# Up and convolution-in projections as seven quarter products each (Strassen's scheme), with the sums of weights made by GpSimd

## Chip, cores and metric

One NeuronCore of a Trainium2 chip runs one program. The metric is the time of the device in microseconds for the whole program, median over runs. Engine names are those of the profile: PE is TensorE's matmul side, PEld its weight loads, DVE is VectorE, ACT is ScalarE, POOL is GpSimd, SP is SyncE, which here only issues the loads of weights.

## What is computed

Two transformer-like layers and the start of a third on 512 tokens of width 1024, all in float32. The parts that the change touches:

```python
# end of layer 1: feed-forward
xn2 = rmsnorm(x, norm2_g[l])
x = x + jnp.square(jax.nn.relu(xn2 @ w_up[l])) @ w_down[l]      # w_up 1024 x 4096
# layer 2: gated short convolution, width 2048
h = rmsnorm_2(x, norm_g)
b, c, u, z = jnp.split(h @ w_in, 4, axis=-1)                    # w_in 1024 x 8192
vp = jnp.pad(c * u, ((0, 0), (CONV_WIDTH - 1, 0), (0, 0)))
conv = conv_w[0] * vp[:, 0:S] + conv_w[1] * vp[:, 1:1 + S] + conv_w[2] * vp[:, 2:2 + S]
x = x + (b * conv * jax.nn.silu(z)) @ w_out
```

Before them stand a dilated attention and a retention (with the input projection of 12,800 columns, two output projections and `w_out`), after them the key, value and query projections and a block-sparse attention of the third layer.

## The kernel before

Activations lie transposed in SBUF: feature on the partition, the 512 tokens along the free dimension (`xT`, eight slices k of 128 features). Every large matrix product is made of three fp32r matmuls: an operand is split into a high part (a rounded copy) and a low part (the value less its high part), and high x high, high x low and low x high are summed in one PSUM bank.

**Weights** come as chunks of 1 MB (128 x 2048 elements in SBUF) in a fixed list, `CHUNKS`. For each chunk SP loads it into one of three `raw` buffers, ACT writes the high part `wh` (`w_` of the scalar part, line 1167), DVE the low part `wl` (`w_` of the vector part, line 1618). `wh` and `wl` have two buffers each. `w_` of a chunk waits until PE has read the chunk that was two earlier (`chunk_read`).

**Products.** A chunk of `w_up` or of the convolution's `w_in` has 1024 rows and 256 columns. It gives two tiles ("col" form) of 128 output features x 512 tokens, each of 8 slices k x 3 matmuls, all of them with 128x128 stationary weights and 512 moving columns (`mm`, line 878). There are 8 chunks in each half of up (f = 0, 1) and 32 in the convolution, in the order c, u, b, z: 48 chunks of 48 matmuls.

**What follows a tile.** In up: DVE takes the relu and multiplies by the norm's factor `rs` out of PSUM (`up`), ACT squares it and writes its high part `hh` (line 1403), DVE writes the low part `hl` (line 1883). In the convolution, per tile: `c_` one DVE operation, `u` four (a product, one tap as a product with a scalar, two taps more), `b_` two, `z` three with a silu on ACT in between and a cast `cyh` on ACT (line 1416).

**Norms.** After each tile of `w_out`, down or the convolution's `w_out`, `add_x` adds it to `xT` and makes the next layer's input: `x * gain` on DVE, `xh` on ACT, `xl` on DVE. The squares' sums pass through a matmul (`sum_squares`) and give `rs`, which multiplies the results afterwards.

**Order.** All engines walk one list, `ORDER`, and each takes its own tokens from it in that order; semaphores (`tell`, `told`) do the rest. An engine that waits therefore holds all of its later tokens. `rooted` puts the norm's root some steps into the first two tiles (`ROOT`). POOL has one kind of token, `rate` (line 2183), in the last attention.

Of the kernel before, what the change touches and what calls it, by code (L numbers as in the profile page):

```python
# [14 lines left out]
S = 512  # L15
# [5 lines left out]
TURN = (1, 4, 4)  # L21
ATT_SCALE = 128 ** -0.5
NSA_SCALE = 64 ** -0.5

VECS = {}
# [6 lines left out]
NVEC = _at  # L32

# [81 lines left out]
def lay_out():  # L115
# [42 lines left out]
    for c in range(4):  # L158
        chunk(("wo", c), "w_out", 0, 8, c * 256, 256)
        for j in range(2):  # L160
            col(("wo", c, j), ("wo", c), j * 128, 8, ("y",), "out_d")
    for f in range(2):
        for c in range(8):
            chunk(("up", f, c), "w_up", 0, 8, f * 2048 + c * 256, 256)
            for j in range(2):
                col(("up", f, c, j), ("up", f, c), j * 128, 8, ("x", 1), "out_d")
        for c in range(8):
            chunk(("down", f, c), "w_down", f * 2048, 16, c * 128, 128)
            col(("down", f, c, 0), ("down", f, c), 0, 16, ("h", f), "out_d")
    for c in range(8):  # L170
        for n, part in ((1, "c"), (2, "u"), (0, "b"), (3, "z")):
            chunk((part, c), "a_w_in_2", 0, 8, n * 2048 + c * 256, 256)
            for j in range(2):
                col((part, c, j), (part, c), j * 128, 8, ("x", 2), "out_d")
# [28 lines left out]
SPLIT = [c[0] for c in CHUNKS if c[6] != "whole"]  # L203
# [14 lines left out]


# [5 lines left out]

def after_chunk(name):

    if name in LATE or name not in AFTER or AFTER[name] in PIECED:
        return []
# [41 lines left out]
def rooted(s, key, after):  # L271
# [5 lines left out]
    return o[:n] + flat(t[:at]) + [("sum_squares", s), ("root", s)] + o[n:] + flat(t[at:])  # L277

# [35 lines left out]
def make_order():  # L314
# [48 lines left out]
    for f in range(2):  # L363
        o += whole(("up", 1, 0, 0), ("up", 1, 0, 1)) if f else rooted(1, ("up", 0, 0, 0), ("up", 0, 0, 1))
        o += whole(*[("up", f, c, j) for c in range(8) for j in range(2)][2:])
        for k in range(8):
            o += whole(("down", f, k, 0)) + (squared(2, k) if f else [])
# [127 lines left out]
ROOT = {1: 5, 2: 4, 3: 0}  # L495
# [123 lines left out]
def program(nc, ctx, a, out):  # L619
# [10 lines left out]
    vec = sb("vec", [128, NVEC])  # L630
# [5 lines left out]
    wh = [sb(f"wh{i}", [128, 2048], F32R) for i in range(NSPLIT)]  # L636
    wl = [sb(f"wl{i}", [128, 2048], F32R) for i in range(NSPLIT)]
    tmp = [sb(f"tmp{i}", [128, S]) for i in range(4)]
    tmp45 = sb("tmp4", [128, 2, S])
    tmp += [tmp45[:, 0, :], tmp45[:, 1, :]]  # L640
# [3 lines left out]
    def v_(name, j=None):  # L644
        lo, hi = VECS[name]
        return vec[:, lo:hi] if j is None else vec[:, lo + j:lo + j + 1]
# [31 lines left out]
    with ExitStack() as ph:  # L678
        hh = sb("hh", [128, 16, S], F32R, ph)
        hl = sb("hl", [128, 16, S], F32R, ph)  # L680
    with ExitStack() as ph:
        cyh = sb("cyh", [128, 16, S], F32R, ph)
        cyl = sb("cyl", [128, 16, S], F32R, ph)
        vp = [sb(f"vp{i}", [128, S + 2], F32, ph) for i in range(2)]
        rs2 = sb("rs2", [128, S], F32, ph)
# [6 lines left out]
    with ExitStack() as ph:  # L692
# [7 lines left out]
        with ExitStack() as ph2:  # L700
            cn = sb("cn", [128, 1280], F32, ph2)
            w2 = sb("w2", [128, 2, 2, 64], F32, ph2)
# [8 lines left out]
    pair = [(sb(f"th{i}", [128, 2 * S], F32R), sb(f"tl{i}", [128, 2 * S], F32R)) for i in range(2)] + [(th2, tl2)]  # L711
    x_mid = nc.dram_tensor("x_mid", (4, 128, D), F32, kind="Internal").ap()
# [18 lines left out]

    XS = {"x": (xh, xl, "xl"), "or": (orh, orl, "orl"), "oa": (oah, oal, "oal"), "y": (yh, yl, "yl"),
# [5 lines left out]
    def new_rings():  # L738
# [5 lines left out]
                     main_n=Ring((7,), held), bo=Ring((0, 1, 2, 3), held))  # L744
# [49 lines left out]

    def x_event(s, k):
        return (("xT", 0, k), ("out_d", ("wo", k // 2, k % 2)), ("out_d", ("down", 1, k, 0)), ("out_d", ("ao", k, 0)))[s]
# [22 lines left out]
    def tensor(e):  # L819
# [27 lines left out]
        def mm(key, k):  # L847
# [33 lines left out]
            elif kk == kn - 1 and LAST[name] == key:  # L881
                m.then_inc(*tell("half", name))

# [255 lines left out]
        follow(x_in, x_raw, sum_squares, mm, turn_qk, scores, probs, values, mix_turn, mix_pick, mix, decay, ret, gated_ret,  # L1139
# [4 lines left out]
    def scalar(e):  # L1144
# [15 lines left out]
        def w_(j):  # L1160
# [3 lines left out]
            if name in BEFORE:  # L1164
                w.wait_ge(*told(*chunk_read(BEFORE[name])))
            for r, hi, _ in split_views(name, raw[SLOT[n]], wh[WSLOT[name]], wl[WSLOT[name]]):
                m = e.copy(hi, r)  # L1167
            m.then_inc(*tell("hi", name))

# [32 lines left out]
        def square(s, k):  # L1202
            w.wait_ge(*told(*x_event(s, k)))
            if k >= 3:
                w.wait_ge(*told("sum_square", s, k - 2))
# [8 lines left out]
            act(tmp[k % 2 if k else 5][:, :], xT[:, k, :], ACT.Square).then_inc(*tell("square", s, k))  # L1214

        def root(s):
# [3 lines left out]
            elif s == 3:  # L1220
                w.wait_ge(*told("out_d", ("z", 7, 1)))
# [163 lines left out]
        def gain(s, k, read):  # L1385
            w.wait_ge(*told("tile", read))
            w.wait_ge(*told("gain", s, k))
            e.copy(xh[:, k, :], tmp[2 + k % 3][:, :]).then_inc(*tell("xh", s, k))  # L1388

        def wo(c, j):  # L1390
            gain(1, c * 2 + j, ("gb", 3, 1))

        def up(f, c, j):
            key, n = ("up", f, c, j), c * 2 + j
            t = tmp[2 + n % 4]
            w.wait_ge(*told("out_d", key))
# [899 lines left out]
```

## Time and profile before

| | |
|---|---|
| median of 3 runs | 2085.94 us (2084.77 to 2087.73) |
| the profiled execution: time, span | 2087.92 us, 2086.1 us |
| mean granted TensorE clock | 0.991 |
| PE busy, matmuls | 2040.1 us (98%), 9591 |
| PEld busy | 1654.3 us (79%) |
| DVE busy | 1021.1 us (49%) |
| ACT busy | 769.2 us (37%) |
| POOL busy | 80.0 us (4%) |

Busy shares are over the whole span. A PE matmul's busy time in the rows overlaps the next one's, so the distance between two starts, not the mean duration, says what one costs. The engine that is busy 98% is waited for by the others in most of the span.

### The profile page before, as it was taken

The page shows a single profiled execution, that of the slowest core. Times are in us where ns is not written, and L with a number is a line of the kernel's source. Part 1 is how long each engine was busy: PE and PEld are TensorE (multiplying, and loading weights), DVE is VectorE, ACT ScalarE, POOL GpSimd, SP SyncE. Part 2 cuts the span into 40 slices and gives each one's busy share as a digit, 9 for nine tenths or more (in the row PEclk, how much of TensorE's full clock was granted, in tenths as well). Part 3 has the DMA queues.
Part 4 walks back from the last instruction along what each step waited for, and adds up shares of the span by engine and source line. Part 5 has one row for each costly group of instructions (what it writes and reads, how often), then busy time and mean ns, then how long its engine had stood idle before and what let it go on. Part 6 is the DMA issues. An engine that isn't in the chain of part 4 may idle for free. (4 is left out here: it accounts for less than half of the span.)

```text
span 2086.1 us, 22886 instructions
## 1 busy us (share of the span) xinstructions
PE 2040.1 (98%) x9591; PEld 1654.3 (79%) x9591; DVE 1021.1 (49%) x1353; ACT 769.2 (37%) x1217; POOL 80.0 (4%) x132
## 2 busy tenths in 40 slices
PE   8999999999999999999999999999999999999897
PEld 6899986778787888888888888888888777766566
DVE  4443444434343346643244455555554454856665
ACT  4564551332323323442143222222222214366763
POOL 0000000000000000000000000000000000033431
PEclk9999998999999999999999999999999999999999
DMA  5222122222222232333323333323333435210002
GB/s 201 73 69 81 61 81 71 81 86 81 86 81 81 81 101 89 93 101 101 101 89 94 101 101 91 103 89 101 101 89 94 124 96 160 65 41 21 31 21 61
DMA packets 186422, 181.32 MB, mean 87 GB/s; under 512 B 4816, under 2 KB 162896, under 8 KB 186320
## 3 DMA queue, kind: packets, MB, share of 16 engines
q1 hardware_dynamic: 182832, 172.41, 26.9%
q10 hardware_dynamic: 3488, 7.45, 1.3%
q8 instruction: 76, 1.25, 0.3%
q14 instruction: 26, 0.21, 0.0%
HBM read 173.56 MB, written 4.19 MB: 85 GB/s over the span
## 5 line engine op out<-in xcount | busy, mean ns | idle before, releaser
L878 PE MATMUL bank<-xh,wh 128*128 128x512 f32 x1352 | 549.4, 406 | 0.9 <-DVE wl L1618 0.8
L878 PE MATMUL bank<-xh,wl 128*128 128x512 f32 x1352 | 529.3, 391 | 0.0
L878 PE MATMUL bank<-xl,wh 128*128 128x512 f32 x1352 | 528.7, 391 | 0.0
L1618 DVE TENSOR_TENSOR wl<-raw,wh 128x2048 fp32r<-128x2048 f32 (+2 forms) x154 | 342.2, 2225 | 324.3 <-ACT wh L1167 324.3
L1167 ACT CAST wh<-raw 128x2048 fp32r<-128x2048 f32 (+2 forms) x154 | 285.1, 1854 | 383.6 <-PE bank L878 382.2
L878 PEld LDWEIGHTS bank<-xh,wh 128*128 128x128 f32 x1352 | 254.5, 188 | 61.6 <-issue 9.9
L878 PEld LDWEIGHTS bank<-xl,wh 128*128 128x128 f32 x1352 | 254.7, 188 | 57.5 <-issue 6.9
L878 PEld LDWEIGHTS bank<-xh,wl 128*128 128x128 f32 x1352 | 254.4, 188 | 54.9
L878 PE MATMUL bank<-wh,xh 128*128 128x512 f32 x512 | 214.4, 419 | 4.8 <-DVE xl L2140 4.6
L878 PE MATMUL bank<-wl,xh 128*128 128x512 f32 x512 | 202.0, 395 | 0.0
L878 PE MATMUL bank<-wh,xl 128*128 128x512 f32 x512 | 202.0, 395 | 0.0
L878 PEld LDWEIGHTS bank<-wh,xh 128*128 128x128 f32 x512 | 120.2, 235 | 18.2 <-issue 6.1
L878 PEld LDWEIGHTS bank<-wh,xl 128*128 128x128 f32 x512 | 120.1, 235 | 13.0
L878 PEld LDWEIGHTS bank<-wl,xh 128*128 128x128 f32 x512 | 121.1, 236 | 11.1 <-issue 0.2
L2183 POOL TENSOR_SCALAR tmp<-tmp,rs 128x128 f32<-128x128 f32 (+3 forms) x88 | 54.1, 627 | 1926.7 <-DVE rs L2104 1926.7
L1151 ACT ACTIVATE tmp<-tmp 128x512 f32<-128x512 f32 (+2 forms) x61 | 36.6, 603 | 194.8 <-DVE tmp L1580 100.6
L878 PE MATMUL bank<-hh,wh 128*128 128x512 f32 x256 | 99.6, 389 | 0.0
L878 PE MATMUL bank<-hl,wh 128*128 128x512 f32 x256 | 99.6, 389 | 0.0
L878 PE MATMUL bank<-hh,wl 128*128 128x512 f32 x256 | 99.6, 389 | 0.0
L1848 DVE TENSOR_TENSOR xT<-xT,bank 128x512 f32<-128x512 f32 x32 | 21.9, 686 | 122.4 <-PE bank L878 122.4
L2113 DVE TENSOR_TENSOR tl<-bank,th 128x512 fp32r<-128x512 f32 (+1 forms) x88 | 52.3, 636 | 42.7 <-ACT th L1524 42.5
L1388 ACT CAST xh<-tmp 128x512 fp32r<-128x512 f32 x24 | 14.9, 620 | 149.9 <-DVE tmp L1857 149.9
(256 smaller groups left out, 2578.8 us busy)
## 6 DMA issues: line engine op xcount, KB each, us to landing
raw<-in_w_in SPq DMA_DIRECT2D x50, 1024.0 KB, 5.1
raw<-in_a_w_in SPq DMA_DIRECT2D x32, 1024.0 KB, 5.7
raw<-in_w_up SPq DMA_DIRECT2D x16, 1024.0 KB, 5.4
raw<-in_w_down SPq DMA_DIRECT2D x16, 1024.0 KB, 6.0
raw<-in_w_proj_b SPq DMA_DIRECT2D x8, 1024.0 KB, 5.1
raw<-in_a_w_out SPq DMA_DIRECT2D x8, 1024.0 KB, 6.0
raw<-in_w_out SPq DMA_DIRECT2D x4, 1024.0 KB, 5.3
raw<-in_w_kv SPq DMA_DIRECT2D x4, 1024.0 KB, 5.1
```

Source lines behind the costliest of these rows:

```text
L878: m = e.matmul(o, p, q, start=k == 0 and n == 0, stop=k == K - 1 and n == 2)
L1151: return e.activation(o, i, f, scale=scale, **kw)
L1167: m = e.copy(hi, r)
L1388: e.copy(xh[:, k, :], tmp[2 + k % 3][:, :]).then_inc(*tell("xh", s, k))
L1618: m = e.tensor_tensor(lo, r, hi, ALU.subtract)
L1848: e.tensor_tensor(xT[:, k, :], xT[:, k, :], tile_bank(key)[:, :], ALU.add).then_inc(*tell("out_d", key))
L2113: e.tensor_tensor(lo[:, o:o + m], bank_of("turn_n", ("turn_n", u, f))[:, 0:m], hi[:, o:o + m], ALU.subtract).then_inc(*tell("lo_n", u, f))
L2183: m = e.tensor_scalar(x, x, wt[:, 32 + c + j:33 + c + j], gts[:, qb, (p * 2 + f) * 4 + i0 + j, 1 + n:2 + n], ALU.mult, ALU.mult)
```

## The change

Each of the 48 chunks is treated as a 2 x 2 block matrix: rows 0 to 511 and 512 to 1023, columns 0 to 127 and 128 to 255. The input is cut likewise: features k < 4 and k >= 4, tokens 0 to 255 and 256 to 511. The product is then made of seven quarter products in Winograd's form of Strassen's scheme with 15 sums. A quarter product has 4 slices k x 3 matmuls with 256 moving columns: 84 matmuls for a chunk.

- Sums of the input (`x_parts`, three of four sums for each k >= 4 and one for each k < 4) are made once per norm, by DVE, and split by ACT and DVE into `xwh`, `xwl`.
- Sums of the weights: four for each chunk, 128x512 elements, by POOL (`ws`) into a new buffer `wsum`. High and low parts are made per product: seven casts of 128x512 on ACT (`wq`) and seven subtractions on DVE (`wl_`). Products lie in a ring of eight places in `wh`, `wl`, `wsum`.
- Sums of the results, 128x256 each: ACT copies out of PSUM (`m1`, `m5`, `m4`), DVE sums (`u2`, `u3`, `c12`, `c11`), POOL sums in SBUF (`u4`, `c22`, `c21`). They build the two tiles in SBUF, and what follows (`up_rs`, `u`, `b_`, `z`) reads them there and not in PSUM.
- The tokens that follow a product come a fixed number of products later (`SEVEN_AT`); the weights are prepared 7, 6 and 5 products ahead.
- The middle tap's product with a scalar goes from DVE to ACT (`tap`). Chunks of `w_out` and the order of down are paired (0, 4, 1, 5, ...), so that slices k and k + 4 come together (`PAIRS`).
- To make room in SBUF six of the eight slices of `xT` are written to DRAM when the convolution begins and read back at its end (`x_keep`, `x_back`). The root of the norm comes after three products. PSUM banks 0 to 6 form the ring of the products.

```diff
-            chunk(("up", f, c), "w_up", 0, 8, f * 2048 + c * 256, 256)
-            for j in range(2):
-                col(("up", f, c, j), ("up", f, c), j * 128, 8, ("x", 1), "out_d")
+            chunk(("up", f, c), "w_up", 0, 8, f * 2048 + c * 256, 256, "seven")
...
+def sevens(r, s=None):
+    run, near = RUNS[r], NEXT_TO[r]
+    Q = 7 * len(run)
...
+    for q in range(7, Q):
+        name, n = product_at(r, q)
+        for what in ("ws", "wq", "wl"):
+            if q >= 8 or what == "wl":
+                due[max(0, q - SEVEN_AT[name[0], what])].append((what, name, n))
...
-    o += rooted(2, ("c", 0, 0), ("c", 0, 1))
-    o += whole(*[(part, c, j) for c in range(8) for part in "cubz" for j in range(2)][2:])
+    o += sevens(2, 2) + [("x_back", n) for n in range(3)]
...
+    for _w, _n in (("ws", 7), ("wq", 6), ("wl", 5), ("m1", 0), ("m5", 1), ("u2", 3), ("u4", 4), ("u3", 5), ("c22", 6), ("c12", 6),
+                   ("c11", 7), ("m4", 7), ("c21", 8), ("up_rs", 9), ("up", 11), ("up_lo", 13), ("u", 9), ("tap", 11),
+                   ("taps", 13), ("b", 9), ("z", 9), ("silu_z", 11), ("cy", 13), ("cyl", 15)):
...
+        def wm(name, n):                                        # PE
...
+            for k in range(4):
...
+                for x, (p, q) in enumerate(((hi, h), (hi, l), (lo, h))):
+                    m = e.matmul(product_bank(name, n), p[:, k, :], q, start=k == 0 and x == 0,
+                                 stop=k == 3 and x == 2)
...
+        def wq(name, n):                                        # ACT
...
+            e.copy(product_weights(name, n)[1], product_source(name, n)).then_inc(*tell("hi", name, n))
...
+        def wl_(name, n):                                       # DVE
+            _, hi, lo = product_weights(name, n)
+            w.wait_ge(*told("hi", name, n))
+            if n in (1, 2):
+                w.wait_ge(*told("rated", name, n + 1))
+            e.tensor_tensor(lo, product_source(name, n), hi, ALU.subtract).then_inc(*tell("lo", name, n))
...
+        def ws(name, n):                                        # POOL
+            if n in (0, 5, 6):
+                return
+            i, o = PLACE[name], product_weights(name, n)[0]
+            w.wait_ge(*told(f"raw{SLOT[i]}", i))
+            w.wait_ge(*told(*place_free(name, n)))
+            if n == 1:
+                m = e.tensor_tensor(o, raw_part(name, 1, 0), raw_part(name, 1, 1), ALU.add)
+            elif n == 2:
+                w.wait_ge(*told("rated", name, 1))
+                m = e.tensor_tensor(o, product_weights(name, 1)[0], raw_part(name, 0, 0), ALU.subtract)
...
+        def u4(name):                                           # POOL
...
+            e.tensor_tensor(t[:, 256:512], u2_sum, m5_copy, ALU.add).then_inc(*tell("rated", name, "u4"))
...
+        def up_rs(f, c, j):                                     # DVE
+            key, t = ("up", f, c, j), tmp[2 + (c * 2 + j) % 4]
+            tile_made(("up", f, c), j)
+            w.wait_ge(*told("rs", 1))
+            stt(t, t, 0.0, rs[:, :], ALU.max, ALU.mult).then_inc(*tell("out_d", key))
```

## Rows read from the trace of the kernel before

**Rows 1.** The page: busy time of each engine.

```profile
PE 2040.1 (98%) x9591; PEld 1654.3 (79%) x9591; DVE 1021.1 (49%) x1353; ACT 769.2 (37%) x1217; POOL 80.0 (4%) x132
```

**Rows 2.** PE's waits, longest in total first, with the longest single one.

```profile
PE bank L833 <- DVE xs L1598: 10.4, 4, 7.8
...
PE bank L878 <- DVE wl L1618: 1.5, 3, 0.7
```

**Rows 3.** Windows of up's first half and the convolution: engines' busy time, clock, DMA.

```profile
859.00:944.30 85.30, 85.01 (x374) 69.73 (x373) 42.22 (x40) 34.85 (x41) 0.00 (x0) 1.00 0.34 97
...
1206.30:1554.40 348.10, 348.10 (x1535) 287.91 (x1534) 184.84 (x197) 82.31 (x66) 0.00 (x0) 1.00 0.33 97
```

**Rows 4.** Timeline of PE, the convolution: start, duration, 512 moving columns.

```profile
1499.78 0.39 PE L878 MATMUL bank<-xl,wh 128*128 128x512 f32 x1
...
1502.96 0.39 PE L878 MATMUL bank<-xh,wh 128*128 128x512 f32 x1
```

**Rows 5.** Timeline of PE, last attention: fp32r matmuls of 256 moving columns.

```profile
2035.22 0.28 PE L1131 MATMUL bank<-th,v 128*128 128x256 f32 x1
...
2037.01 0.28 PE L1131 MATMUL bank<-tl,v 128*128 128x256 f32 x1
2037.13 0.39 PE L878 MATMUL bank<-wh,xh 128*128 128x512 f32 x1
```

**Rows 6.** Groups of DVE by shape: count, busy us, mean ns, idle before.

```profile
L1618 DVE TENSOR_TENSOR wl<-raw,wh 128x2048 fp32r<-128x2048 f32 x145 | 332.2, 2291 | 313.7 <-ACT wh L1167 313.7
...
L1883 DVE TENSOR_TENSOR hl<-tmp,hh 128x512 fp32r<-128x512 f32 x32 | 22.1, 692 | 43.3 <-ACT hh L1403 43.3
...
L2058 DVE TENSOR_TENSOR tmp<-tmp,rs 128x256 f32<-128x256 f32 x8 | 3.4, 425 | 0.3
```

**Rows 7.** Groups of ACT by shape.

```profile
L1167 ACT CAST wh<-raw 128x2048 fp32r<-128x2048 f32 x145 | 276.6, 1907 | 382.3 <-PE bank L878 382.2
...
L1403 ACT CAST hh<-tmp 128x512 fp32r<-128x512 f32 x32 | 19.9, 621 | 1.1
...
L1151 ACT ACTIVATE tmp<-tmp 128x256 f32<-128x256 f32 x8 | 3.3, 418 | 30.6 <-DVE tmp L2058 30.6
```

**Rows 8.** Timeline of POOL: its operation undisturbed, two of 128x512, eight of 128x128.

```profile
1910.09 1.53 POOL L2183 TENSOR_SCALAR tmp<-tmp,rs 128x512 f32<-128x512 f32 x2 [2.39 <-DVE rs L2104]
...
1843.53 3.44 POOL L2183 TENSOR_SCALAR tmp<-tmp,rs 128x128 f32<-128x128 f32 x8 [1843.09 <-DVE rs L2104]
```

**Rows 9.** Timeline of POOL and DVE where both work, four places.

```profile
1937.60 1.88 POOL L2183 TENSOR_SCALAR tmp<-tmp,rs 128x512 f32<-128x512 f32 x2 [4.13 <-DVE rs L2104]
...
1937.41 0.67 DVE L1624 TENSOR_TENSOR wl<-raw,wh 128x512 fp32r<-128x512 f32 x1
1938.00 1.28 DVE L2096 TENSOR_REDUCE rs<-bank 128x4 f32<-128x512 f32 x2
...
2045.37 2.40 POOL L2183 TENSOR_SCALAR tmp<-tmp,rs 128x512 f32<-128x512 f32 x2 [2.42 <-DVE rs L2104]
...
2045.19 1.27 DVE L1624 TENSOR_TENSOR wl<-raw,wh 128x512 fp32r<-128x512 f32 x2
...
1953.65 4.31 POOL L2183 TENSOR_SCALAR raw<-raw,rs 128x128 f32<-128x128 f32 x8 [1.95 <-DVE rs L2104]
...
1954.75 0.75 DVE L2134 TENSOR_TENSOR oT<-oT 128x512 f32<-128x512 f32 x1
1956.74 0.90 DVE L2140 TENSOR_TENSOR xl<-oT,xh 128x512 fp32r<-128x512 f32 x1 [1.24 <-ACT xh L1548]
...
1909.91 1.26 DVE L2096 TENSOR_REDUCE rs<-bank 128x1 f32<-128x512 f32 x2
```

**Rows 10.** Timeline of DVE where the convolution's input is made.

```profile
1205.80 0.69 DVE L1848 TENSOR_TENSOR xT<-xT,bank 128x512 f32<-128x512 f32 x1 [4.28 <-PE bank L878]
1206.52 0.49 DVE L1857 TENSOR_SCALAR tmp<-xT,vec 128x512 f32<-128x512 f32 x1
1207.69 0.69 DVE L1859 TENSOR_TENSOR xl<-tmp,xh 128x512 fp32r<-128x512 f32 x1 [0.69 <-ACT xh L1388]
```

More of the change, by code:

```diff
@@ L158, in lay_out @@
     for c in range(4):
[L159 removed]
+        chunk(("wo", c), "w_out", 0, 8, c * 128, 256, "far")
         for j in range(2):
@@ L171, in lay_out @@
         for n, part in ((1, "c"), (2, "u"), (0, "b"), (3, "z")):
-            chunk((part, c), "a_w_in_2", 0, 8, n * 2048 + c * 256, 256)
-            for j in range(2):
-                col((part, c, j), (part, c), j * 128, 8, ("x", 2), "out_d")
+            chunk((part, c), "a_w_in_2", 0, 8, n * 2048 + c * 256, 256, "seven")
     for c in range(8):
@@ L202 @@
 PLACE = {c[0]: n for n, c in enumerate(CHUNKS)}
-SPLIT = [c[0] for c in CHUNKS if c[6] != "whole"]
+SPLIT = [c[0] for c in CHUNKS if c[6] not in ("whole", "seven")]
 SLOT = []
@@ L277, in rooted @@
     return o[:n] + flat(t[:at]) + [("sum_squares", s), ("root", s)] + o[n:] + flat(t[at:])
+PIECES = ("m1", "m5", "u2", "u4", "u3", "c22", "c12", "c11", "m4", "c21")
+POST = {"up": ("up_rs", "up", "up_lo"), "c": (), "u": ("u", "tap", "taps"), "b": ("b",),
+        "z": ("z", "silu_z", "cy", "cyl")}
+def sevens(r, s=None):
+    run, near = RUNS[r], NEXT_TO[r]
+    Q = 7 * len(run)
+    due = [[] for _ in range(Q + 30)]
+    for i, name in enumerate(run):
+        for what in PIECES:
+            due[7 * i + SEVEN_AT[name[0], what]].append((what, name))
+    if s is not None:
+        due[ROOT[s]] += [("sum_squares", s), ("root", s)]
+    for q in range(7, Q):
[3 more added lines that the diff above has]
+                due[max(0, q - SEVEN_AT[name[0], what])].append((what, name, n))
+    due[Q - 4].append(("w", NTH[near[2]]))
+    due[Q].append(("w", NTH[near[3]]))
+    for i, name in enumerate(run):
+        for what in POST[name[0]]:
+            for j in range(2):
+                due[7 * i + SEVEN_AT[name[0], what] + j].append((what, *name[1:], j))
+    return flat([([("wm", *product_at(r, q))] if q < Q else []) + due[q] for q in range(Q + 30)])
 def placed(seq, extra):
@@ new lines, in tap, with silu_z @@
+        def tap(c, j):
+            f = c * 2 + j
+            w.wait_ge(*told("cu", c, j))
+            w.wait_ge(*told("rs", 2))
+            w.wait_ge(*(told("cyl", f - 4) if f >= 4 else told("xl", 2, 11)))
+            act(tmp[2 + f % 4], vp[j][:, 2:], ACT.Copy, scale=v_("a_conv_w_2", 32 + f)).then_inc(*tell("out_a", "tap", f))
+        def silu_z(c, j):
+            w.wait_ge(*told("out_d", ("z", c, j)))
+            act(two[:, j, :], two[:, j, :], ACT.Silu).then_inc(*tell("z_silu", c * 2 + j))
```

419 lines of the change are left out of this document (311 added, 108 removed).

## Prediction

> **What bounds the kernel now.** I read the page first: PE is busy 98% of the span, no other engine more than half [rows 1]. Because a busy PE says little by itself, I read its waits next. The longest is 10.4 us and lies at the start of the program; for the splits of weights PE waits 1.5 us in all [rows 2]. Then the windows of the two stretches that the change touches. In up's first half and in the convolution the busy time of PE equals the window (85.0 of 85.3 us, 348.1 of 348.1) at a granted clock of 1.00, DVE is busy for half of it (42.2 and 184.8 us), ACT for 41% and 24%, POOL not at all [rows 3]. So these stretches, 48 chunks of weights, last as long as PE needs for its matmuls, and about 5 us per chunk lie free on DVE and all of the time on POOL. DMA engines are busy a third [rows 3], and the change loads the same weights.
>
> The timeline gives what one matmul costs: from 1499.78 to 1502.96 us stand 15 starts, 14 distances, 0.227 us each [rows 4]. The whole convolution gives the same: 348.1 us for 1536 matmuls, 0.2266. A chunk is 48 of them, 10.88 us, and the 48 chunks are 522 us, a quarter of the time. Nothing else of the program is meant to change.
>
> **PE's side of the change.** A chunk becomes 84 matmuls with 256 moving columns, each with its own weight load. The last attention has such matmuls, fp32r too: from 2035.22 to the next matmul at 2037.13 us there are 16, 0.1194 us each [rows 5]. Half the columns cost 53% of the time, since each matmul has a fixed part. 84 x 0.1194 = 10.03 us, which is 0.85 us less than now for a chunk and 41 us less for 48. Bounds: with half of the 0.2267 (no more fixed part than now per column) a chunk is 9.52 us; the 0.1194 was seen in bursts of 16 alone, and the gain is gone at 10.88 / 84 = 0.1295. I take 0.1194.
>
> **ACT's side.** Per chunk seven casts of 128x512 at 0.62 us [rows 7] are 4.3 us in place of one of 1.91. Copies out of PSUM of 256 columns have no row; the 256-column activation takes 0.42 [rows 7], three are 1.3 (I would take 0.3 to 0.6 each). Up adds two squares and two casts as now, 2.5 us, the convolution per chunk a half tap, a half silu and a half cast, under 1 us. Sum 8.1 us in up and under 7 in the convolution: below PE's 10.0, so ACT costs nothing as long as nobody holds it up; it is the thinner cover in up.
>
> **DVE's side.** Per chunk seven subtractions of 128x512 in place of one of 2.29 us. One lasts 0.69 us by its row [rows 6], but the next begins earlier: from 1937.41 to 1938.00 it is 0.59 [rows 9]. Seven are 4.1 us. Four sums of 128x256, 0.43 each [rows 6], 0.34 where they follow at once: 1.4 us. In up two times `up_rs` and `up_lo`, 2.4 us at 0.59. Sum 7.9 us (9.3 with the rows' full durations). In the convolution nine operations of 128x512 follow each of the two tiles of four chunks, 4.5 per chunk, 2.7 us: sum 8.2. DVE alone would be under 10.03 as well.
>
> **POOL's side.** Per chunk four sums of 128x512 and three of 128x256, each with two inputs. The trace has only its one-input operation: 1.53 us for two of 512, 3.44 for eight of 128, so 0.76 and 0.43 each [rows 8], that is a fixed 0.32 us and 0.86 ns per element. Lower bound of a two-input sum: the same, 0.76 for 512 and 0.54 for 256, 4.7 us per chunk. Upper bound: the second input is read after the first at the same rate, 1.20 and 0.76, 7.1 us per chunk. I take the upper one, for the row's per-element time is one element per step and these sums need two. POOL too is under 10.03.
>
> **Where it collides.** Each engine fits, but two of them don't fit together. The timeline shows POOL's operations beside DVE's. Beside reductions out of PSUM two of them take 1.53 us. Where a DVE subtraction with both inputs in SBUF has begun just before (1937.41), they take 1.88; where two such stand in a row from 2045.19 to 2046.46, they take 2.40, 0.88 more, which is the rest of DVE's pair (1.09 us from POOL's start at 2045.37) less 0.2 that still overlaps. And eight small ones stretch from 3.44 to 4.31, while DVE's two two-input operations in the same stretch take 0.75 and 0.90 in place of 0.69 [rows 8, 9]: both sides lost, 1.1 us together, about the length of the two DVE operations. The two engines take turns when both read SBUF and DVE has two inputs there. The Trainium skill says this as a rule (SBUF — State Buffer, "Who interferes with whom": a DVE instruction with two SBUF inputs contends with a GpSimd instruction that reads SBUF, and the second to start blocks in full); by this rule, the trace agrees at all the places that I looked at.
>
> So the sum to make is of turns. DVE in up: seven `wl_`, two `up_rs`, two `up_lo`, all with both inputs in SBUF (`up_rs` read PSUM before), 11 x 0.59 = 6.5 us; in the convolution 11.5 x 0.59 = 6.8 us. `u2`, `u3`, `c12`, `c11` read PSUM and don't count. POOL's seven: 7.1 us, less 0.15 each that overlapped in rows 9, gives 6.0. Sum of turns: 12.5 us in up, 12.8 in the convolution, against 10.03 that PE would need and 10.88 that it needs now. Perfect turns are not likely: `c12` on DVE waits for `u4` on POOL with the later `wl_` queued behind it, `ws` on POOL waits for its predecessor, `u4` for `u2` on DVE. I add 0.5 us, about a third of the four PSUM sums: 13.0 and 13.3 us per chunk. Bounds: with the cheap POOL sums (4.7 less 1.0) the turns are 10.2 to 10.5 us, below the 10.88 of now, PE nearly the bound; with 7.1 whole and DVE's four PSUM sums never beside POOL, 6.8 + 7.1 + 1.4 = 15.3 us.
>
> The Trainium skill has a price for POOL's sum (GPSIMD Engine Reference, "Performance versus the Vector engine"): 4.50 us for 2048 elements of two inputs. An estimate from that page, in proportion to the elements, is 1.12 us for 512 and 6.2 for a chunk's seven; no row here shows it, and with it the turns would be 0.9 us shorter per chunk and the forecast 43 us lower, 2160.
>
> **Between the runs.** `x_parts` makes for the last pair a gain, three sums of 256, ACT's casts of 768 and 512 and DVE's two subtractions. Now the chain from the last tile to `xl` is 2.6 us (1205.80 to 1208.38) [rows 10]; the new one is about 0.7 + 0.5 + 3 x 0.4 + 0.85 + 0.9 = 4.2. Products 0 and 1 need only k < 4 and cover 2.9 us; the third waits some 1.5 us, twice in the program. At the start and end of each run the weights of four products wait for the last chunk of the old kind: 0 to 2 us, three times. I take 6 us for all of it, bounds 2 and 15. The 1.5 MB to DRAM and back cost nothing: the DMA engines are a third busy [rows 3], nobody reads `xT` meanwhile, and the reload has the first tile of `w_out`, 10.9 us, before its sum needs it; if late by 4 us, DVE's slack in that stretch (half) takes it.
>
> **Sum.** Up 16 x 13.0 = 208, convolution 32 x 13.3 = 426, together 634 us against 522: +112, and +6 makes +118. On the profiled execution of 2087.9 us (span 2086.1 and 1.8 around it) that is 2206, and since it was 2 us above the median of the runs, I predict 2203 us.
>
> **Rivals.**
> - *Faster: PE stays the bound.* The turns cost little, because DVE's and POOL's waits fall into the 2 us that each has free, or POOL's sums are cheap. For it: each engine alone is under 10.03 us, and the weights are prepared 5 to 7 products (7 to 10 us) ahead, so single delays are absorbed. Against it: a lead absorbs delays, not a rate. It decides where the turns sum to less than 10.0, that is POOL's seven under 3.5 us or DVE's lock well under 0.59. Time: 2087.9 - 41 + 6 - 2 = 2051. Chance 0.17.
> - *Near a tie.* POOL's sums at the cheap bound with 0.5 us lost in turns, 10.2 + 0.5 to 10.5 + 0.5: about -3 us for up and +4 for the convolution, with the edges 2093; or PE's short matmuls at 0.13 in a long stream. Chance 0.05, of which 0.02 within 0.2%.
> - *POOL is starved.* DVE always has the next two-input operation ready and POOL gets in only when DVE waits (at 2045 POOL did not get in between two of them [rows 9]); DVE then waits for `u4` each time with nothing running beside. 15.3 us per chunk: 48 x (15.3 - 10.88) = +212, 2304 with the edges. Chance 0.10.
> - *The forecast*, the turns bind at 12 to 14.5 us per chunk: +54 to +174, 2146 to 2266 with the edges. Chance 0.68.
>
> The range has to hold eight in ten: the forecast's, the tie's slower side and half of the starved case. 2090 to 2290. Faster 0.18, the same 0.02 (within 0.2%, 4 us, about what a measurement of this kernel tells from no change), slower 0.80. The likeliest one's own range is 2146 to 2266.
>
> **What the profile after would show.** Right: matmuls of 256 columns start 0.12 us apart within a product, but PE waits between products for `wl_` of DVE, busy share near 80% in these stretches; `ws` of POOL lasts over 1.2 us on average and scatters, `wl_` lasts over 0.69 in the mean; DVE and POOL together are never both idle for long. The other stretches are as long as before. Wrong: PE waits for nothing and a chunk lasts 10.0 us (no turns), `ws` of 0.76 us, or PE's starts more than 0.13 us apart inside a product (the fixed part of a matmul is larger in a long stream). If PE waited long enough for its clock to fall to 1.2 GHz, the window's granted clock would say so; with waits of a few microseconds at most I count nothing for it.

## The result and the profile after

The changed kernel takes 2222.98 us (median of 4 runs, 2222.37 to 2224.22) against 2086.84 us for the kernel before beside it (4 runs, 2084.77 to 2090.7): ratio 1.0651, 95% interval 1.0632 to 1.0669. It is 6.5% slower. The forecast was 2203 us with a range of 2090 to 2290.

The page of the changed kernel, against [rows 1]:

```profile
PE 2042.6 (92%) x11319; PEld 1723.9 (78%) x11319; DVE 1416.2 (64%) x1857; ACT 927.0 (42%) x1673; POOL 541.2 (24%) x468
```

By the page PE is busy for as long as before, in a span 135 us longer, though its matmuls should need some 40 us less. The loss stands at PE's waits. Against [rows 2] (in total, times, longest):

```profile
PE bank L1025 <- DVE wl L1822: 110.2, 90, 2.1
...
PE bank L1025 <- DVE xl L2126: 4.5, 1, 4.5
PE bank L1005 <- DVE tmp L1842: 4.0, 1, 4.0
```

Ninety waits of 1.2 us in the mean for `wl_` make 110 us, and none is over 2.1: a queue that is short of rate, not one late event. The windows of up's first half, of most of its second and of the convolution, against [rows 3] (PE, PEld, DVE, ACT, POOL busy, then the clock):

```profile
862.80:971.20 108.40, 88.55 (x665) 83.69 (x665) 104.77 (x122) 58.39 (x108) 68.49 (x51) 0.97 0.27 79
1061.00:1165.00 104.00, 91.11 (x700) 87.03 (x701) 102.11 (x115) 57.61 (x106) 70.74 (x53) 1.00 0.32 92
1246.00:1686.00 440.00, 348.35 (x2692) 334.07 (x2691) 430.79 (x499) 185.96 (x367) 303.60 (x219) 0.98 0.26 78
```

DVE went from half busy to 97 or 98%, PE from 100% to 79 to 88%. An engine that was busy for half of the time before is the bound now. What it spends the time on is in its groups by shape, against [rows 6]:

```profile
L1822 DVE TENSOR_TENSOR wl<-wsum,wh 128x512 fp32r<-128x512 f32 x192 | 179.5, 941 | 1.4 <-POOL wsum L2471 1.2
L1822 DVE TENSOR_TENSOR wl<-raw,wh 128x512 fp32r<-128x512 f32 x144 | 175.1, 1237 | 5.3 <-ACT wh L1319 5.3
...
L2147 DVE TENSOR_TENSOR hl<-tmp,hh 128x512 fp32r<-128x512 f32 x32 | 33.7, 1053 | 2.5 <-ACT hh L1590 2.5
...
L2199 DVE TENSOR_TENSOR cyl<-tmp,cyh 128x512 fp32r<-128x512 f32 x16 | 26.1, 1639 | 0.1
```

`hl` is the same instruction as before and lasts 1053 ns in the mean instead of 692. DVE waits for nobody (last column); its instructions are longer. POOL's groups say where the extra time lies:

```profile
L2476 POOL TENSOR_TENSOR wsum<-raw 128x512 f32<-128x512 f32 x48 | 82.1, 1711 | 20.2 <-PE bank L1005 20.2
...
L2474 POOL TENSOR_TENSOR wsum<-raw,wsum 128x512 f32<-128x512 f32 x48 | 73.9, 1539 | 11.4 <-PE bank L1025 5.0
...
L2492 POOL TENSOR_TENSOR two<-tmp 128x256 f32<-128x256 f32 x24 | 27.0, 1126 | 25.1 <-DVE tmp L1842 25.1
```

The timeline of the two engines at one place in up (start, duration), DVE first, then POOL in the same microseconds, against [rows 8, 9]:

```profile
899.97 3.45 DVE L1822 TENSOR_TENSOR wl<-raw,wh 128x512 fp32r<-128x512 f32 x2
...
903.96 0.41 DVE L1833 TENSOR_TENSOR tmp<-tmp,bank 128x256 f32<-128x256 f32 x1
904.29 0.68 DVE L1822 TENSOR_TENSOR wl<-wsum,wh 128x512 fp32r<-128x512 f32 x1
904.89 1.22 DVE L1776 SCALAR_TENSOR_TENSOR tmp<-tmp,rs 128x512 f32<-128x512 f32 x1
906.04 1.76 DVE L1822 TENSOR_TENSOR wl<-wsum,wh 128x512 fp32r<-128x512 f32 x1
...
899.65 1.54 POOL L2471 TENSOR_TENSOR wsum<-wsum,raw 128x512 f32<-128x512 f32 x1
901.33 1.55 POOL L2474 TENSOR_TENSOR wsum<-raw,wsum 128x512 f32<-128x512 f32 x1
904.50 1.07 POOL L2485 TENSOR_TENSOR tmp<-tmp 128x256 f32<-128x256 f32 x1 [1.62 <-issue]
905.53 1.72 POOL L2476 TENSOR_TENSOR wsum<-raw 128x512 f32<-128x512 f32 x1
```

A DVE subtraction that has begun before POOL's sum takes 0.68 us (904.29), and POOL's of 256, begun at 904.50, pays with 1.07 in place of 0.74 (about the smallest duration of these sums). The next one of DVE (904.89) stands behind that sum and takes 1.22. Behind a sum of 512 it is 1.7 (899.97, two in 3.45; 906.04). The DVE sum that reads PSUM lasts 0.41, as the 48 of its kind do in the mean. And POOL is stretched too: from 899.65 to 903.36, 3.7 us, two POOL sums and two DVE subtractions were done, 1.85 us for each pair. POOL's sum with nothing beside it is 1.27 to 1.30 us (its smallest durations), DVE's own pitch 0.59 [rows 9]: 1.88. At this place they alternate, one instruction each.

PE itself, against [rows 4, 5]: within a product its matmuls start 0.12 us apart, and each chunk of up has two waits for `wl_`. After longer waits it is slow for a while:

```profile
901.89 0.36 PE L1025 MATMUL bank<-xwh,wh 128*128 128x256 f32 x1 [1.25 <-DVE wl L1822]
902.08 0.28 PE L1025 MATMUL bank<-xwl,wh 128*128 128x256 f32 x1
...
907.95 0.36 PE L1025 MATMUL bank<-xwh,wh 128*128 128x256 f32 x1 [1.17 <-DVE wl L1822]
...
915.18 0.36 PE L1025 MATMUL bank<-xwh,wh 128*128 128x256 f32 x1 [1.25 <-DVE wl L1822]
...
971.27 0.78 PE L1005 MATMUL bank<-hh,wh 128*128 128x512 f32 x1 [2.74 <-DVE tmp L1848]
971.86 0.63 PE L1005 MATMUL bank<-hl,wh 128*128 128x512 f32 x1
...
974.41 0.55 PE L1005 MATMUL bank<-hl,wh 128*128 128x512 f32 x1
974.80 0.39 PE L1005 MATMUL bank<-hh,wl 128*128 128x512 f32 x1
```

From wait to wait a chunk of up is 915.18 - 901.89 = 13.29 us. That is 3.2 us more than its 84 matmuls need without a gap, 1.6 for each of the two waits. (The profile's 1.25 counts from the modelled end of the matmul before; from start to start it is 1.5 us, and the next distance or two are longer as well.) The convolution's 32 chunks are 439.8 us, 13.74 each with the waits at start and end in it. From 971.86 to 974.4 the matmuls of 512 columns start 0.43 us apart in place of the 0.227 of [rows 4], which is the clock's lower level, 1.2 GHz (granted clock 0.51 from 971.3 to 974.8); it rose at about 974.8.

Two windows in the steady state, one chunk of up and four of the convolution:

```profile
894.65:907.94 13.29, 10.86 (x84) 10.29 (x85) 13.29 (x16) 7.36 (x15) 9.80 (x7) 1.00 0.27 79
1291.24:1345.90 54.66, 42.53 (x338) 40.79 (x338) 53.78 (x63) 24.37 (x47) 38.71 (x29) 1.00 0.26 78
```

DVE is busy for all of the 13.29 us and for 98% of the 54.66. The convolution repeats every four chunks, so its steady price is 54.66 / 4 = 13.67 us.

Where the 135 us lie, by the first and the last matmul on `hh`, and the first on `cyh`: before 944.5, 1204.9 and 1554.6, after 971.3, 1245.6 and 1686.1. Up and its down stages +40.7, the convolution +90.8, all that comes later +3.5.

### The profile page after: what moved, and what is told of

It reads as the page before. It is cut to its first block and busy times, and to the rows that moved or that the text cites. A ratio compares the mean times of both kernels' runs of the same rounds, so it can differ in the third digit from the quotient of the medians.

```text
span 2221.1 us, 28525 instructions
## 1 busy us (share of the span) xinstructions
PE 2042.6 (92%) x11319; PEld 1723.9 (78%) x11319; DVE 1416.2 (64%) x1857; ACT 927.0 (42%) x1673; POOL 541.2 (24%) x468
## 5 line engine op out<-in xcount | busy, mean ns | idle before, releaser
L1814 DVE TENSOR_TENSOR wl<-raw,wh 128x2048 fp32r<-128x2048 f32 (+1 forms) x106 | 233.6, 2207 | 279.8 <-ACT wh L1312 279.5
L1025 PE MATMUL bank<-xh,wh 128*128 128x256 f32 x768 | 226.3, 295 | 47.5 <-DVE wl L1822 41.2
L1312 ACT CAST wh<-raw 128x2048 fp32r<-128x2048 f32 (+1 forms) x106 | 193.4, 1828 | 174.4 <-PE bank L1005 172.7
L1005 PE MATMUL bank<-xh,wh 128*128 128x512 f32 (+1 forms) x584 | 249.6, 427 | 1.0 <-issue 0.5
L1005 PE MATMUL bank<-xh,wl 128*128 128x512 f32 (+1 forms) x584 | 230.5, 395 | 0.0
L1005 PE MATMUL bank<-xl,wh 128*128 128x512 f32 (+1 forms) x584 | 230.1, 394 | 0.0
L1025 PE MATMUL bank<-xl,wh 128*128 128x256 f32 x768 | 220.4, 287 | 0.0
L1025 PE MATMUL bank<-xh,wl 128*128 128x256 f32 x768 | 220.1, 287 | 0.0
L1822 DVE TENSOR_TENSOR wl<-wsum,wh 128x512 fp32r<-128x512 f32 x192 | 179.5, 941 | 1.4 <-POOL wsum L2471 1.2
L1822 DVE TENSOR_TENSOR wl<-raw,wh 128x512 fp32r<-128x512 f32 x144 | 175.1, 1237 | 5.3 <-ACT wh L1319 5.3
```

The lines of the kernel that those rows point to most:

```text
L1005: m = e.matmul(o, p, q, start=k == 0 and n == 0, stop=k == K - 1 and n == 2)
L1025: m = e.matmul(product_bank(name, n), p[:, k, :], q, start=k == 0 and x == 0, stop=k == 3 and x == 2)
L1814: m = e.tensor_tensor(lo, r, hi, ALU.subtract)
L1822: e.tensor_tensor(lo, product_source(name, n), hi, ALU.subtract).then_inc(*tell("lo", name, n))
```

## The experiments

The kernels that were run. The time is the median, or the one run; the last column is, in the profiled execution, the time from the last `hh` matmul to the first of `cyh`, that is the convolution's 32 chunks with their start and end. The kernel before ran beside each: 2089.7 us beside the kernels without weight sums, with fills, with PSUM and without POOL, 2087.9 beside the two steps between and the two with other values, 2087.4 beside the last.

| kernel | time, us | convolution, us |
|---|---|---|
| before | 2086.8 | 349.7 |
| changed | 2223.0 | 440.5 |
| weight sums left out | 2070.7 | 329.2 |
| sums replaced by fills | 2107.6 | 353.2 |
| `wl_` reads PSUM | 2117.4 | 370.7 |
| results' sums on DVE | 2204.9 | 431.9 |
| and two of the weight sums | 2185.1 | 412.3 |
| and all of them, no POOL | 2150.6 | 390.9 |
| half of the conv chunks plain (values differ) | 2083.7 | 341.1 |
| a quarter plain (values differ) | 2129.3 | 386.4 |
| half plain, with x's difference in buffers of its own | 2085.6 | 341.5 |

**Weight sums left out.** POOL does no weight sum, products 1 to 4 take a raw quarter of the weights; PE's, ACT's and DVE's instructions are the same in number and size.

```
-        return raw_part(name, *{0: (0, 0), 5: (0, 1), 6: (1, 1)}[n]) if n in (0, 5, 6) else product_weights(name, n)[0]
+        return raw_part(name, *((0, 0), (1, 0), (1, 1), (0, 1), (0, 0), (0, 1), (1, 1))[n])
...
-        follow(ws, u4, c22, c21, rate)
+        follow(u4, c22, c21, rate)
```

> The four sums of weights per chunk are left out: the products that need a sum take a plain quarter of the weights in its place, so the values differ; every other instruction of PE, ACT and DVE stays, POOL keeps its three sums of results. Theory of turns (DVE operations with two inputs in SBUF and POOL operations that read SBUF exclude each other): 11 x 0.59 us of DVE and 3 x 0.9 us of POOL are 9.2 us per chunk, under PE's 10.03, so PE binds, about 2055 us, and the mean subtraction wl falls from over 1 us towards 0.7. Theory that DVE's own work is too much (it has as many instructions as after): stays at 2200 or more. Theory that short matmuls are slower in a long stream: 2100 or more with PE busy.

2070.74 us, one run. The window of the convolution:

```profile
1250.00:1530.00 280.00, 280.00 (x2335) 280.00 (x2335) 266.03 (x431) 155.24 (x317) 89.83 (x84) 1.00 0.35 104
```

PE is the bound again, without a gap, at 2335 matmuls in 280 us, 0.1199 us each: 84 are 10.07 us. So the seven products give what was worked out on PE, and ACT keeps up. Only 16 to 19 us of it arrive, though (against 2086.8, and against the 2089.7 beside it), where 48 x (10.88 - 10.07) would be 39; the time is 16 us over the 2055 that were expected. The timeline of PE at up's start shows where some of the rest goes:

```profile
863.83 0.39 PE L1025 MATMUL bank<-xh,wh 128*128 128x256 f32 x1 [2.00 <-DVE xl L2124]
...
868.60 0.39 PE L1025 MATMUL bank<-xwh,wh 128*128 128x256 f32 x1 [1.64 <-DVE xwl L2120]
...
870.53 0.41 PE L1025 MATMUL bank<-xl,wh 128*128 128x256 f32 x1
870.75 0.41 PE L1025 MATMUL bank<-xh,wl 128*128 128x256 f32 x1
```

Two waits and one of 0.6 us (869.80), and then 0.21 us a matmul, the lower clock, from 870.3 to 873.6 (granted 0.50). The first wait stands inside product 0, the second inside product 2, each before the last slice, k = 3. DVE's chain to the new operands is longer than what products 0 and 1 cover, and product 0 itself is held up. From 874 to 1658 the granted clock is 1.00.

**Sums replaced by fills.** In place of each weight sum POOL fills the same buffer three times with zero, each after the other, so that it is as busy as with a sum or more; products 1 to 4 so compute with zero weights.

```
-                m = e.tensor_tensor(o, raw_part(name, 1, 0), raw_part(name, 1, 1), ALU.add)
...
+            for x in range(3):
+                m = e.memset(o, 0.0)
+                if x < 2:
+                    m.then_inc(*tell("filled", name, n, x))
+                    w.wait_ge(*told("filled", name, n, x))
```

> Each of POOL's four sums of weights is replaced by three fills of the same 128x512 place with zero, each waiting for the one before: POOL is busy about as long and its results come about as late, but it reads nothing there; values differ. Theory of turns: fills don't exclude DVE, PE binds, 2055 to 2075 us, and DVE's subtractions take about 0.7 us. Theory that POOL is late by its own rate and latency (its results come too late for ACT and DVE, whatever DVE does): 2180 or more.

2107.64 us, one run, 115 below the changed kernel and 33 over the upper end of what was expected from turns alone. Groups of POOL and of DVE:

```profile
L2470 POOL MEMSET wsum<- 128x512 f32 x576 | 303.7, 527 | 1051.3 <-PE bank L1005 1013.9 <-PE bank L1025 4.6
...
L1822 DVE TENSOR_TENSOR wl<-wsum,wh 128x512 fp32r<-128x512 f32 x192 | 151.4, 791 | 63.9 <-POOL wsum L2470 43.5 <-ACT wh L1319 20.4
L1822 DVE TENSOR_TENSOR wl<-raw,wh 128x512 fp32r<-128x512 f32 x144 | 105.9, 752 | 7.0 <-ACT wh L1319 4.2
```

Twelve fills of 0.53 are 6.3 us of POOL per chunk, more than four undisturbed sums (5.2), and DVE's subtraction is back at 752 ns (1237 before this edit; 755 in the kernel without weight sums). Most of the loss, 115 of 136 us, is not POOL's being busy but its reading its inputs while DVE reads two. What is left against the kernel without sums, 37 us, goes with POOL's rate and chain: DVE now waits 43.5 us for it, PE 20.3 us for `wl_`. That part of the rival theory holds.

**`wl_` reads PSUM.** The subtraction takes its second input from an unused PSUM bank in place of `wh` (so `wl` holds other values), and the products go round six banks. Everything else of DVE, and POOL's sums, stay.

```
-            e.tensor_tensor(lo, product_source(name, n), hi, ALU.subtract).then_inc(*tell("lo", name, n))
+            e.tensor_tensor(lo, product_source(name, n), banks[6][:, :].rearrange("p (k c) -> p k c", k=4), ALU.subtract).then_inc(
+                *tell("lo", name, n))
```

> The seven subtractions of weights per chunk on DVE take their second input from a PSUM bank that holds other data and not from wh in SBUF (values differ; six banks are left for the products). DVE has the same instructions of the same length, with one SBUF input. POOL's sums are all there. Theory of turns: only 4 to 4.5 DVE operations per chunk still collide with POOL's seven, and the subtractions, beside a sum or not, take 0.7 us each: DVE 7.9 us of its own and 2 to 3 us of being held up, 10 to 11 us per chunk, 2060 to 2110 us. Theory of POOL's rate or of DVE's load: 2180 or more.

2117.39 us, one run, 7 over the expected range. DVE's groups, and POOL's instructions on `wsum` (duration smallest/median/largest, ns):

```profile
L1822 DVE TENSOR_TENSOR wl<-raw,bank 128x512 fp32r<-128x512 f32 x144 | 96.7, 682 | 20.0 <-ACT wh L1319 17.6
L1776 DVE SCALAR_TENSOR_TENSOR tmp<-vp,vec,tmp 128x512 f32<-128x512 f32 x32 | 38.8, 1213 | 0.6
...
L2164 DVE TENSOR_TENSOR vp<-vp,rs 128x512 f32<-128x512 f32 x16 | 26.7, 1668 | 0.5
```

```profile
L2469 POOL TENSOR_TENSOR wsum<-raw x48: 1276/1296/1755, 845.0 to 1556.7; 128x512 f32<-128x512 f32 x48
...
L2477 POOL TENSOR_TENSOR wsum<-raw x48: 1281/1300/1753, 856.9 to 1562.9; 128x512 f32<-128x512 f32 x48
```

With one input from PSUM the subtraction takes 682 ns (679 where it follows a sum), in the midst of POOL's sums; the operations that still have both inputs in SBUF stay slow (1213 ns where the changed kernel has 1290, 1668 where it has 1173). This is the sharpest of the tests: same engines, same counts, same element counts, only the place of one input (and one bank less for the products). Freeing seven of DVE's eleven two-input operations gave back 106 of 136 us, and two of POOL's four sums are down to 1.30 in the median.

**No POOL at all.** DVE takes the results' sums from PSUM (`u4`, `c22`, `c21`; the copies `m5` and `m4` go) and the four weight sums, in the same places of the order. This is the rival way to do the change.

```
-        follow(ws, u4, c22, c21, rate)
+        follow(rate)
...
+            e.tensor_tensor(t[:, 256:512], u2_sum, product_bank(name, 1), ALU.add).then_inc(*tell("out_d", name, "u4"))
...
+                m = e.tensor_tensor(o, raw_part(name, 1, 0), raw_part(name, 1, 1), ALU.add)
```

> All sums from POOL go to DVE: the four of weights (0.59 us each), and the three of results, which read the product's PSUM bank there, so that two copies on ACT fall away. The result is the full one. Theory of turns: a sum of 128x512 on POOL costs DVE 1.1 us of being held up (1.69 us from start to start in place of 0.59), on DVE it costs 0.59, so the kernel gets faster although POOL is idle: DVE 7.9 + 4 x 0.59 + 3 x 0.34 = 11.3 us in up and 11.6 in the convolution, DVE is the bound, 552 us for the 48 chunks against 652, about 2125 us. Theory that DVE is overloaded as it is: seven more operations per chunk make it slower than 2223 us.

2150.60 us (2147.33 to 2153.46), ratio 1.0297, 1.0268 to 1.0325. It is 72 us faster than with POOL's help. A weight sum takes DVE 0.6 us when it does it itself, and holds it up by 1.1 when POOL does it and it meets a two-input operation of DVE in full. But DVE alone is then the bound: 11.34 us per chunk in up, 12.2 in the convolution (390.9 / 32) with its start and end, 11.98 in its steady state. So the kernel missed the 2125 us that were expected by 25; 12 of them are the 0.38 us by which the convolution's chunks are dearer than the 11.6 worked out, and where the rest lies was not measured. The window of the convolution and the subtraction:

```profile
1246.00:1606.00 360.00, 321.96 (x2549) 318.92 (x2548) 355.50 (x673) 159.20 (x283) 0.00 (x0) 0.95 0.29 88
```

```profile
L1810 DVE TENSOR_TENSOR wl<-raw,wh 128x512 fp32r<-128x512 f32 x144 | 100.0, 696 | 4.1 <-ACT wh L1322 2.8
```

**The steps between.** First only the results' sums go to DVE and POOL keeps the four weight sums; then DVE does two of those as well.

```
-        follow(ws, u4, c22, c21, rate)
+        follow(ws, rate)
...
-            if n in (0, 5, 6):
+            if n not in (2, 3):
                 return
```

> POOL keeps its four sums of weights; its three sums of results go to DVE, which reads the product's PSUM bank there (one SBUF input), and two copies on ACT fall away. Full result. Theory of turns with the prices seen so far: each of POOL's 256-wide sums held DVE up for about 0.55 us, on DVE it costs 0.34, so 0.6 us less per chunk at most, 2190 to 2215 us. If the result's chain over three engines (u2 on DVE, u4 on POOL, c12 on DVE) was the loss, and not the turns: 2150 or less, near the kernel without POOL.

> As the one before, and two of the four sums of weights (n = 1 and 4) on DVE as well, two on POOL. Theory of turns: each sum that stays on POOL holds DVE up by 1.1 us and spares it 0.59, so the time lies between the kernel with four sums on POOL and the one with none (2150.6), about halfway. Theory that sharing the sums balances the two engines: below 2150, near 2110.

2204.89 and 2185.12 us, one run each, both as the turns would have it: neither the results' chain over three engines nor an even sharing of the sums was what was lacking. From four weight sums on POOL over two to none it goes 2205, 2185, 2151: 20 and 35 us for 96 sums each, monotone, and not quite halfway in the middle (2178). Each sum is cheaper on DVE, by 0.2 and 0.36 us. That is less than the 0.5 of 1.1 less 0.6, and fits what a chunk of up shows: of the 7.4 us that POOL's seven sums take alone, DVE is held up for 13.29 - 7.9 = 5.4, so not all of a POOL sum meets a two-input operation. None of these mixtures reaches the kernel before.

**Fewer chunks by seven.** If DVE's 12.2 us per seven-product chunk is the bound and a plain chunk needs 5.1 us of it (four subtractions and 4.5 operations of 0.6), alternate chunks should bring DVE to 8.7 us per chunk, under PE's mean of 10.5. From the kernel without POOL: up by plain products, and of the convolution's chunks every second one, or every fourth one, plain.

```
+PLAIN = {name for run in RUNS for i, name in enumerate(run) if name[0] == "up" or i % 2}
+PRODUCTS = [[(name, n) for name in run for n in range(4 if name in PLAIN else 7)] for run in RUNS]
...
+                    for x, (p, q) in enumerate(((hi, h), (hi, l), (lo, h))):
+                        m = e.matmul(bank_of("sevens", (name, n // 2 * 2))[:, :], p[:, k, :], q,
+                                     start=n % 2 == 0 and k == 0 and x == 0, stop=n % 2 == 1 and k == 3 and x == 2)
```

In both, the plain chunks of the convolution read, for the second half of the sequence and the first four slices, the difference that the seven products keep there, so the values are not the full result that the expectations speak of; the instructions are the same in number and size.

> No sums on POOL. Up is computed with eight quarter products as in the kernel before (the weights in pieces of 128x512, the tile copied out of PSUM by ACT); of the convolution every second chunk (u and z) too, the other 16 chunks by seven products. Full result. DVE per pair of chunks: 12.2 us for the seven and about 5.5 for the plain one, 17.7, against 10.08 + 10.88 = 20.96 us of PE: PE is the bound again. Gain 16 x 0.8 = 12.8 us less the stalls at the start and the end of the convolution, 2 + 2 us: 2078 us, 0.4% faster than before. If DVE's bursts on the seven-product chunks exceed the lead of five products: 2090 or more.

> As the one before, with only the u chunks computed by eight quarter products and 24 chunks by seven. DVE per four chunks 3 x 12.2 + 5.5 = 42.1 us, PE 3 x 10.08 + 10.88 = 41.1: DVE is the bound by a little, 8 x 42.1 = 337 us against 348 of before, less the stalls: 2079 us, no better than with half of the chunks. If DVE's 12.2 us per chunk holds only while it is the bound everywhere, 2072.

Half: 2083.69 us (11 runs, 2080.01 to 2087.76), ratio 0.998, 0.9972 to 0.9989, a gain of 0.2% where 0.4% was expected. Three of four: 2129.28 us (2127.53 to 2130.02), ratio 1.0197, 1.0183 to 1.0211, far from the 2072 to 2079 that was expected. The sum of the expectation, about as much DVE work as PE work in the mean, doesn't explain that: with 12.0 us for the seven and 5.1 for the plain chunk DVE needs 330 us for the 32 chunks, about what PE needs, and 386 were measured. What PE's timeline shows:

```profile
1304.79 0.39 PE L1051 MATMUL bank<-xh,wh 128*128 128x256 f32 x1 [4.16 <-DVE two L1855]
...
1306.23 0.41 PE L1051 MATMUL bank<-xl,wh 128*128 128x256 f32 x1
1306.44 0.41 PE L1051 MATMUL bank<-xh,wl 128*128 128x256 f32 x1
...
1309.50 0.28 PE L1051 MATMUL bank<-xh,wl 128*128 128x256 f32 x1
```

```profile
DVE wl L1840 <- ACT wh L1345: 40.2, 8, 5.4
```

```profile
1206.00:1588.00 382.00, 344.62 (x2389) 325.18 (x2387) 329.76 (x602) 162.25 (x287) 0.00 (x0) 0.96 0.29 89
```

A wait of 4.2 us for DVE to free a bank, and 1.2 us later the matmuls start 0.21 us apart for 3.2 us. PE idles 37 us of the 382 and has a mean clock of 0.96. DVE is busy for 86% and idle for 40 us in eight waits of 5 us, one at each plain chunk, for ACT's high part of the next weights (the line on `wl`: total, times, longest, from 1206 to 1590). ACT gives that late because its copy of the plain tile stands before it and waits for PE, 3.8 us for the copy at 1326.12. So DVE can't work ahead while the plain chunk runs, and over the three chunks by seven it falls behind by more than the banks hold. That the order of ACT's tokens is the cause is read from the trace; no run with another order was made.

**Half, with the values right.** The difference needs buffers of its own, 8 KB a partition, which are free only once the last slice of x has gone to DRAM. So the plain chunk comes first (`c` and `b` plain, `u` and `z` by seven), all eight slices are copied out, and `rs2` gives way to a second multiplication by `rs`.

```
+        def xa(k):
+            w.wait_ge(*told("xh", 2, 20 + k))
+            stt(xdl[:, k, :], x_diff(k), v_("a_norm_2", k), xdh[:, k, :], ALU.mult, ALU.subtract).then_inc(*tell("xl", 2, 20 + k))
```

> Up all by plain products; in the convolution's chunks c and b plain, u and z by seven products; no GpSimd; all eight slices of x go to DRAM, and the difference of x's two halves has buffers of its own, made at the start of the conv stage (four DVE differences, four ACT casts, four DVE rests) while the first, plain chunk runs. In the earlier kernel of this kind the plain conv chunks read that difference in place of the second half of x, which changes values but no instruction's length. Theory that engines' rates decide: DVE has about 17% of the conv stage free in the earlier kernel and takes some 14 us more here (16 multiplications by rs of 0.69 and the eight small operations), so PE stays the bound: 2083 us, between 2080 and 2086, ratio to before about 0.998. Rival, that the start of the stage decides: the first plain chunk waits for nothing new, but x's last copy to DRAM and the new buffers hold back its result; each microsecond of PE wait there comes on top, 2086 to 2092, ratio 1.000 to 1.002, and shows as a wait of PE at about 1210.

2085.57 us (11 runs, 2084.42 to 2089.4) against 2087.36 (15 runs): ratio 0.9993, 0.9983 to 1.0003. The window in the middle of the stage and the first matmul behind it:

```profile
1250.00:1350.00 100.00, 100.00 (x625) 90.46 (x624) 86.52 (x154) 45.59 (x82) 0.00 (x0) 1.00 0.32 96
```

```profile
1547.34 0.79 PE L1023 MATMUL bank<-cyh,wh 128*128 128x512 f32 x1 [3.29 <-DVE two L1929]
1547.93 0.63 PE L1023 MATMUL bank<-cyl,wh 128*128 128x512 f32 x1
```

This is inside the expected 2080 to 2086; near the stage's start PE waits once, 1.5 us (1226.04). PE has no gap in the middle, and the convolution is 8.2 us shorter of 12.8 possible (16 x 0.80); the stage's end takes a part back, a wait of 3.3 us. In the profiled executions 4.6 us are lost behind the first matmul on `cyh`, with the lower clock at their start, and 1.9 between the first and the last matmul on `hh`. What arrives can't be told from no change. It is the best form of the idea that was found, and it gains nothing measurable.

## Why the prediction was right, and where it was off

- *PE's side.* Taken 0.1194 us a matmul; 0.1199 in a stream of 2335. Right: the short bursts of [rows 5] spoke for the long stream.
- *ACT.* Taken as hidden; with the sums away PE never waited for it in these stages. Right.
- *DVE's own work.* 7.9 and 8.2 us plus seven sums moved there make 4 x 0.6 + 3 x 0.34 = 3.4 more, 11.3 and 11.6; the kernel without POOL needs 11.34 and, in the steady state, 11.98. Right in up, 0.4 short in the convolution.
- *POOL's prices.* Taken from the upper bound, 1.20 and 0.76; alone they take 1.27 to 1.30 and 0.74. The estimate from the Trainium skill (GPSIMD Engine Reference, "Performance versus the Vector engine") was 1.12 for 512; the runs show it too low at this size, and its forecast of 2160 further off than the one by rows. The cheap bound, on which "Near a tie" hung, was ruled out.
- *The turns.* The step that carried the forecast. 13.0 and 13.3 us a chunk were forecast, 13.29 and 13.67 measured in the steady state. POOL's seven at their true prices are 7.4 us and not 7.1, which is about the 0.3 of up. 16 x 0.29 + 32 x 0.37 = 16.5 us, nearly the whole 17 by which the difference of the profiled executions (135 against 118) was missed. The 0.5 us added for imperfect turns was a guess of the right size with a reason that is half right: no DVE subtraction queues behind a wait, DVE is busy for the whole 13.29 us. It is POOL that idles, 3.2 us before three of its result sums (1.6 before `u4`, which needs `u2`; 1.0 before `c22`, which needs `u3`; 0.6 before `c21`, which needs ACT's copy), and two of DVE's four PSUM sums (0.33 each) fall there and not beside a POOL sum. The rule of the Trainium skill (SBUF — State Buffer, "Who interferes with whom") holds in each point that was tried: a DVE operation with both inputs in SBUF collides with a POOL sum, one with a PSUM input doesn't (682 ns), and beside fills, which read nothing, the subtraction takes 752.
- *"Faster: PE stays the bound".* Its argument, that the lead of 7 to 10 us absorbs the delays, fails as the prediction said: 90 waits of 1.2 us. *"POOL is starved"* fails too. The two alternate one by one at the places read, so POOL got its turn even where DVE always had the next operation ready. Why it did not get in between the two subtractions of [rows 9] at 2045, which ran undisturbed in 1.27 us, no run shows.
- *The edges.* The prediction had 6 us, bounds 2 and 15. Where nothing else binds, in the kernel without weight sums, they are larger: counted from the first matmul on `yh` (815.1 to 2068.9, before 811.5 to 2086.1) it is 20.8 us shorter, of 38.9 that PE saves, so 18 are lost. By the same marks as above they lie in up's first half (7.2), the down stages and up's second half (1.4), the convolution (5.4) and all that comes later (4.1). The waits there were mis-sized (2.0, 1.6, 2.2 us and some under 1), above all the one inside product 0, which the prediction took as covered. The lower clock was counted at nothing; up to the end of the convolution it came once, at 870.3, and can have cost at most 1.7 us. In the changed kernel 16 x 2.41 + 32 x 2.79 = 128 of the 135 us are the turns (13.29 and 13.67 less 10.88), which leaves 7 for the edges, near the 6. That nearness is partly luck: up's first half loses 26.8 us, 7.5 more than the 8 x 2.41 = 19.3 of its turns, and its second 13.9, 5.4 less. Weights that are prepared ahead may let a stage begin faster than the turns; that was not tested.
- *x to DRAM and back.* Right: after the convolution DVE waits once, 7.0 us, for the reload, and PE's later stages lose 3.5 us in all.

What stays open is how the 3.5 us after the convolution divide between waits and clock, and why up's second half does not show the loss of its first.

## What to carry to other kernels

Before giving POOL a two-input operation to relieve DVE, count it as DVE time: where they meet it holds DVE's two-input operations up by 1.1 us for 128x512, where DVE would need 0.6 to do it itself. Over whole kernels each weight sum moved from POOL to DVE gained 0.2 to 0.36 us. Sum the turns against the bound, not each engine by itself. Here a saving of 7% on PE more than doubled DVE's work for the chunk (5.1 to 12.0 us). It pays only where DVE's mean stays well below PE's and DVE can work ahead, and then the start and end of each stage, where the new operands have a longer chain, can take it all back.

## What the runs showed that I had not expected

- A single DVE instruction of 128x512 lasts 1.69 to 1.82 us when a POOL sum stands before it, and POOL's next sum waits for it in turn: at the places read they alternate one by one, 1.85 us a pair, with neither engine idle between them by the profile. The time in which one holds the other up counts as busy (98% and 69% in the convolution); only the durations show it.
- Moving one input of the subtraction to PSUM frees it fully, 1237 to 682 ns, in the midst of the same POOL sums.
- A wait of a few microseconds costs PE more than its length. Behind the waits of 2.7 us (971.27), 4.5 (862.81) and 4.0 (1686.11) of the changed kernel and of 3.3 in the last experiment (1547.34) the matmuls started at 1.2 GHz's distance for 3 to 6 us, some 1.4 to 2.5 us lost on top of each.
- Short waits can do it too. In up, behind waits of 1.2 us, the clock stayed up (granted 1.00 from 884 to 965). In the middle of the convolution it fell four times, at 1456, 1511, 1620 and 1674, where PE had waited no longer than 2.1 us at a time. Two waits and the stretch behind them:

```profile
1451.03 0.36 PE L1025 MATMUL bank<-xh,wh 128*128 128x256 f32 x1 [1.36 <-DVE wl L1822]
...
1454.45 0.36 PE L1025 MATMUL bank<-xwh,wh 128*128 128x256 f32 x1 [1.76 <-DVE wl L1822]
```

```profile
1456.00:1459.40 3.40, 3.40 (x19) 3.40 (x18) 3.37 (x4) 0.00 (x0) 3.26 (x3) 0.50 0.01 2
```

  It cost nothing here, because DVE was the bound: each four chunks took 54.7 us all the same. And it is no rule: the same two waits at 1341.7 and 1345.1 were not followed by it (granted 1.00 from 1300 to 1455).
